# Order of loads and of the modulation pieces at the start of a two-block network turned round

## The reference, cut to what matters

```
s_lat = silu(c);  s_ctx = silu(c_ctx)
sh1, sc1, g1, sh2, sc2, g2 = split(s_lat @ w_mod + b_mod, 6)      # 6 x 1024
csh1, csc1, ...            = split(s_ctx @ w_mod + b_mod, 6)
h  = rms_norm(x,   norm1_g) * (1 + sc1)  + sh1
hc = rms_norm(ctx, norm1_g) * (1 + csc1) + csh1
y  = token_mixers(h, hc, ...)      # h @ w_in, hc @ w_in: attention, a hyena branch, differential attention
x  = x + g1 * y
x  = x + g2 * conv_glu(modulate(rms_norm(x, norm2_g), sh2, sc2), ...)
# hyena filters, from positions alone:
f = sin(freq * (z @ fw1 + fb1)); f = sin(freq * (f @ fw2 + fb2)); f = (f @ fw3 + fb3) * decay, normalised, to spectra
# differential attention: lam = exp(lam_q1 . lam_k1) - exp(lam_q2 . lam_k2) + lam_init
```

## Time and profile before

| | |
|---|---|
| median of 3 runs | 2349.61 us (2344.91 to 2351.23) |
| profiled execution | 2351.88 us, its span 2349.9 us |
| TensorE busy | 2199.5 us, 94% of the span |
| VectorE, ScalarE, GpSimd busy | 1209.5, 429.9, 470.2 us |
| mean granted TensorE clock | 0.960 of full speed |
| first projection matmul | at 58.36 us |

### The profile page before, as it was taken

The page is one execution under the profiler, slowest core; times in us unless marked ns, Lnnn a source line. Parts: engine busy times, 40 slices in busy tenths (PEclk is TensorE's granted clock), DMA queues, the critical chain, the costliest instruction groups (busy, mean ns, idle before and its releaser), DMA issues. The chain is left out here.

```text
span 2349.9 us, 32587 instructions
## 1 busy us (share of the span) xinstructions
PE 2199.5 (94%) x13344; PEld 1962.8 (84%) x13344; DVE 1209.5 (51%) x2470; ACT 429.9 (18%) x1034; POOL 470.2 (20%) x410
## 2 busy tenths in 40 slices
PE   4999779998998999999999998998999999999998
PEld 2466468887667899999999998667899999999998
DVE  2045521112532597887744443542597787844443
ACT  2113320000232112442200000232112443200000
POOL 0000000000000012554433331000012444533331
PEclk7999989999987999999999999997999999999999
DMA  8216213343331378999999995431378999999996
GB/s 334 74 71 249 108 54 142 136 153 135 143 135 54 144 268 338 384 384 392 410 409 409 395 406 222 181 144 54 120 257 338 382 392 386 407 409 409 407 406 252
DMA packets 113525, 616.38 MB, mean 262 GB/s; under 512 B 10201, under 2 KB 10585, under 8 KB 95322
## 3 DMA queue, kind: packets, MB, share of 16 engines
q1 hardware_dynamic: 55578, 403.31, 43.8%
q0 software_dynamic: 57504, 208.82, 23.2%
q10 hardware_dynamic: 288, 2.10, 0.3%
HBM read 612.16 MB, written 2.03 MB: 261 GB/s over the span
## 5 line engine op out<-in xcount | busy, mean ns | idle before, releaser
L390 PE MATMUL psum<-HT,arena 128*128 128x160 f32 (+1 forms) x5984 | 994.3, 327 | 15.5 <-DVE HT L1632 7.1
L390 PEld LDWEIGHTS psum<-HT,arena 128*128 128x128 f32 x5984 | 925.5, 192 | 68.7 <-issue 18.1
L390 PE MATMUL psum<-arena 128*128 128x160 f32 (+6 forms) x5850 | 882.2, 313 | 36.4 <-DMA arena<-in_peer_v 14.4
L390 PEld LDWEIGHTS psum<-arena 128*128 128x128 f32 (+2 forms) x5850 | 817.1, 193 | 85.9 <-issue 32.3
L1950 DVE SCALAR_TENSOR_TENSOR arena<-arena,small 128x1024 f32<-128x1024 f32 x180 | 231.2, 1285 | 293.2 <-DMA arena<-in_peer_v,small 285.9
L2050 POOL DMA_INDIRECT arena<-in_peer_u,small x192 | 245.7, 1279 | 317.7 <-DVE small L1901 280.9
L2050 POOL DMA_INDIRECT arena<-in_peer_v,small x192 | 210.6, 1097 | 357.9 <-PE psum L390 209.3
L1901 DVE CUSTOM_DVE_ANT_0 arena<-arena 128x1024 f32<-128x1024 f32 x192 | 228.1, 1221 | 51.6 <-DMA arena<-in_peer_u,small 45.8
L2056 POOL DMA_DIRECT2D row_tokens<-arena x2 | 1.2, 624 | 1118.9 <-ACT arena L957 1118.9
L390 PE MATMUL psum<-arena,HT 128*128 128x384 f32 (+3 forms) x544 | 202.8, 533 | 17.6 <-ACT HT L1009 10.7
L390 PEld LDWEIGHTS psum<-arena,HT 128*128 128x128 f32 x544 | 108.1, 201 | 105.4 <-issue 48.5
(11 more groups left out here) (226 smaller groups left out, 1003.7 us busy)
## 6 DMA issues: line engine op xcount, KB each, us to landing
arena<-in_peer_ut SPq DMA_DIRECT2D x64, 2048.0 KB
arena<-in_peer_v SPq DMA_DIRECT2D x64, 2048.0 KB
arena<-in_w_mod SPq DMA_DIRECT2D x12, 2048.0 KB
arena<-in_w_in SPq DMA_DIRECT2D x16, 1536.0 KB
arena<-in_w_up SPq DMA_DIRECT2D x11, 2048.0 KB
arena<-in_peer_wq SPq DMA_DIRECT2D x8, 2048.0 KB
arena<-in_w_out SPq DMA_DIRECT2D x6, 2048.0 KB
arena<-in_w_down SPq DMA_DIRECT2D x11, 1024.0 KB
```

What stands on the lines that cost most here:

```text
L390: return pe.matmul(o, a, b, start=start, stop=stop, skip_group_check=True)
```

## The change

The kernel computes the same values. What is different is order, in five places.

1. **Loads.** SP now issues `c`, `cols`, then the first `w_mod` tile, `fw1` and `fw2`, the second tile, `x`, the constants, the third tile, `ctx`, the fourth; `rows`, `fw3`, `decay` and `dft` come behind the first `w_in` tile and `gains` behind the second.
2. **Modulation.** TensorE takes the scales first (tiles 2, 3) and the shifts last (0, 1); `ssx` and `ssc` stand between them.
3. **VectorE** normalises x (`normed_stream(0)`) before the first filter's sine argument and before the shifts, and forms the lambda numbers behind both.
4. **ScalarE** adds the shifts to HT before the second sine, and no longer after it.
5. **Waits.** `h_ready` is now raised for each chunk of HT, and the first projection job waits chunk by chunk; the filter's loads have semaphores of their own (`filters_in` for fw1 and fw2, `windows_in`, `rows_in`).

```diff
@@ TensorE @@
-            pe.wait_ge(s("consts_in"), 16)
-            pe.wait_ge(s("x_squared"), 1)
-            square_sums("ssx", 0)
-            pe.wait_ge(s("ctx_squared"), 1)
-            square_sums("ssc", 1)
             pe.wait_ge(s("silu_c_ready"), 1)
...
+            modulation_rows(2)
+            modulation_rows(3)
+            pe.wait_ge(s("consts_in"), 16)
+            pe.wait_ge(s("x_squared"), 1)
+            square_sums("ssx", 0)
+            filter_1()
+            modulation_columns(2)
+            modulation_columns(3)
             modulation_rows(0)
-            filter_1()
+            pe.wait_ge(s("ctx_squared"), 1)
+            square_sums("ssc", 1)
             modulation_rows(1)
             modulation_columns(0)
-            modulation_rows(2)
             modulation_columns(1)
-            modulation_rows(3)
-            modulation_columns(2)
-            modulation_columns(3)
             filter_2()
-            pe.wait_ge(s("h_ready"), 1)
...
-                    token_job(f"zx{t}{b}", w, HT, b, 0, width)
+                    token_job(f"zx{t}{b}", w, HT, b, 0, width, (s("h_ready"), 0) if (t, b) == (0, 0) else None)
@@ ScalarE @@
+            modulation_row(2)
+            act.wait_ge(s("x_in"), 16)
+            act.activation(SQ[:, 0, :, :], XT[:, :, :], ACT.Square).then_inc(s("x_squared"), 1)
+            modulation_row(3)
+            act.wait_ge(s("consts_in"), 16)
+            root("sq_rooted", rstd[:, 0, :], lambda: jobs.wait_read(act, "ssx"))
+            act.wait_ge(s("ctx_in"), 16)
+            act.activation(SQ[:, 1, :, :], CT[:, :, :], ACT.Square).then_inc(s("ctx_squared"), 1)
             modulation_row(0)
+            root("sq_rooted", rstd[:, 1, :], lambda: jobs.wait_read(act, "ssc"))
+            sine(1, F1)
             modulation_row(1)
-            sine(1, F1)
-            modulation_row(2)
-            modulation_row(3)
-            sine(2, F2)
...
+            jobs.wait_read(act, "mod0")
+            jobs.wait_read(act, "mod1")
             shifted(0, HT, 0)
+            sine(2, F2)
             shifted(1, HC, 0)
+            act.wait_ge(s("lam_dots"), 1)
+            act.activation(lam[:, 2:4], lam[:, 0:2], ACT.Exp).then_inc(s("lam_exps"), 1)
@@ VectorE @@
-            sine_argument(1, "fb1")
-            for t in range(4):
-                modulation(t)
+            dve.wait_ge(s("consts_in"), 16)
+            mean_square("ssx", 0)
+            modulation(2)
+            modulation(3)
             jobs.wait_read(dve, "mod3")
             for n in range(2):
                 gain_and_scale(n, "n1g", 8, n)
             normed_stream(0, HT, XT, 0, 0)
+            mean_square("ssc", 1)
+            sine_argument(1, "fb1")
+            modulation(0)
+            modulation(1)
+            normed_stream(1, HC, CT, 1, 1)
             dve.wait_ge(s("sine_out"), 1)
             sine_argument(2, "fb2")
-            normed_stream(1, HC, CT, 1, 1)
+            jobs.wait_read(dve, "f2")
+            lambda_dots()
             filter_windows()
+            lambdas()
@@ SyncE @@
             for n, tile in enumerate(one):
                 stream(tile, one[n - WSLOTS], tile["src"])
+                if n == 0:
+                    load(FW1[0:33, :], ins["hy_fw1"], "filters_in")
+                    load(FW2[0:64, :], ins["hy_fw2"], "filters_in")
+                if n == 1:
+                    load(XT[:, :, :], ins["x"], "x_in")
+                    load(KON[:, :], ins["consts"], "consts_in")
                 if n == 2:
+                    load(CT[:, :, :], ins["ctx"], "ctx_in")
+                if n == 4:
+                    load(RP[:, :], ins["rows_1"], "rows_in")
...
```

More of the change, by code:

```diff
@@ L447, in filter_3 @@
                 pe.wait_ge(s("sine_out"), 2)
+                pe.wait_ge(s("windows_in"), 48)
                 for b in range(TB):
@@ L505, in _ @@
                 if c0 >= Q_COLS:
-                    pe.wait_ge(s("h_ready"), 2)
+                    pe.wait_ge(s("h_ready"), KC + 1)
                     for b in range(TB):
@@ L657, in up @@
                 w = w.rearrange("p (k n) -> p k n", k=KC)
-                channel_job(f"fa{f}", w, HT, [0, P], range(4), (s("h_ready"), 2) if f == 0 else None)
+                channel_job(f"fa{f}", w, HT, [0, P], range(4), (s("h_ready"), KC + 1) if f == 0 else None)
                 used_up.append(tile)
@@ L963, in free @@
                 return psum_free[jobs.where[name][0]]
[L966 to L970, removed]
-            act.activation(CE[:, :, :], CS[:, :, :], ACT.Exp, scale=-1.0).then_inc(s("silu_exp"), 1)
[L972 to L976, removed]
+            act.wait_ge(s("params_in"), 32)
+            act.activation(CE[:, :, :], CS[:, :, :], ACT.Exp, scale=-1.0).then_inc(s("silu_exp"), 1)
             def modulation_row(t):
                 jobs.wait_full(act, f"modr{t}")
-                if t >= 2:
-                    jobs.wait_full(act, f"mod{t - 2}")
+                if t not in (2, 3):
+                    jobs.wait_full(act, f"mod{t + 2 if t < 2 else t - 2 if t > 5 else t - 4}")
                 act.activation(mod_rows(t), bank(f"modr{t}")[:, :], ACT.Copy).then_inc(free(f"modr{t}"), 1)
@@ L1302, in _ @@
             steps(dve.memset(base[:, :], 0.0))
[L1303 to L1307, removed]
             dve.wait_ge(s("silu_exp"), 1)
@@ L1312, in _, with lambda_dots, lambdas @@
             dve.tensor_tensor(CE4[:, :, 0:2], CE[:, :, :], CS[:, :, :], ALU.mult).then_inc(s("silu_c_ready"), 1)
-            dve.wait_ge(s("lam_exps"), 1)
-            steps(dve.tensor_tensor(lam[:, 4:5], lam[:, 2:3], lam[:, 3:4], ALU.subtract))
-            steps(dve.tensor_scalar(lam[:, 5:6], lam[:, 4:5], LAM_INIT, -1.0, ALU.add, ALU.mult))
-            mean_square("ssx", 0)
-            mean_square("ssc", 1)
+            def lambda_dots():
+                dve.wait_ge(s("rows_in"), 16)
+                steps(dve.tensor_tensor(HTMP[:, 0, 0:HD], RP[:, 0:HD], RP[:, HD:2 * HD], ALU.mult))
+                steps(dve.tensor_tensor(HTMP[:, 1, 0:HD], RP[:, 2 * HD:3 * HD], RP[:, 3 * HD:4 * HD], ALU.mult))
+                dve.tensor_reduce(lam[:, 0:2], HTMP[:, 0:2, 0:HD], AX.X, ALU.add).then_inc(s("lam_dots"), 1)
+            def lambdas():
+                dve.wait_ge(s("lam_exps"), 1)
+                steps(dve.tensor_tensor(lam[:, 4:5], lam[:, 2:3], lam[:, 3:4], ALU.subtract))
+                steps(dve.tensor_scalar(lam[:, 5:6], lam[:, 4:5], LAM_INIT, -1.0, ALU.add, ALU.mult))
             def sine_argument(n, bias):
@@ L1337, in filter_windows @@
             def filter_windows():
-                dve.wait_ge(s("filters_in"), 16 * 5)
+                dve.wait_ge(s("windows_in"), 48)
                 for b in range(TB):
```

21 lines of the change are left out of this document (8 added, 13 removed).

## The result

The changed kernel took 2331.9 us in the median of six runs, the kernel before 2352.8 in six on the same chip; the ratio is 0.9902, 95% interval 0.9876 to 0.9928, so 23 us less (17 to 29). One of the six runs of the changed kernel, of 5868.94 us, counts in no ratio and has no explanation here; the median of the other five is 2330.32. The forecast was 18 us. The profiled execution has a span of 2320.8 us against 2349.9, 29.1 less, at the edge of what the runs allow. Both the 18 and the surplus have to be explained.

A forecast was written before the change was run, and what follows sets the result against it. TensorE is busy 94% of the span, so the first projection's start sets the time. Loads 7.3 us plus chain 11.0 gave 18.4, rounded to 18 off the median 2349.61: 2331.6 us, range 2325.6 to 2340.6.

The forecast's parts named there:

- The start carries everything behind it: First projection on TensorE, at 58.36 us: bringing it forward moves more than 2290 us of later work as one piece.
- Loads in order, 7.3 us: Load queue delivers in order of issue; last w_mod tile lands at 32.2 instead of 39.52 us, 7.3 us earlier.
- rival 2: Load queue shares its rate among all issued transfers, first tile lands near 27 us; gain 10, 2339.5 us; chance 0.06.
- The chain, 11.0 us: From last w_mod tile's landing to first projection, over the engines: 7.8 us instead of 18.8, gaining 11.0.
- The copy behind the sine, a new wait: ScalarE's copy of tile 1's rows queues behind the first sine: ready at 36.1, made from 37.5 to 38.1 us.
- `filter_3` not waited for: TensorE's filter_3 needs the second sine, ready at 47.2 us; the zx0 jobs ahead end at 49.7 at the earliest.
- The clock: TensorE's start jobs: gain 24.0 us at full clock, 9.8 at half; first projection pair kept at 13.64 us.
- The mixed sum: TensorE's start jobs partly at full, partly at half clock, tile 0's rows at 2.8 us; gain 18.4 us.
- Rival 1: TensorE at half clock through most of the start; gain 8 to 14 us, near 2339; chance 0.13.
- rivals 3 and 4: Behind the start: 3, an unseen wait hands gain back, chance 0.12; 4, half clock in projections, up to 2370 us, 0.04.
- The size: Whole kernel: 18.4 us gained at the first projection, rounded down to 18, for a median of 2331.6 us.

The follow-up runs named there:

- loads-alone kernel: Kernel before with rows, fw3, decay, dft loaded behind the first w_in tile, gains behind the second, lambda numbers later; other order old; ratio 0.9962.
- after: First profile of the changed kernel, no further edit: first projection at 39.74 us, span 2320.8 us; timed ratio 0.9902.
- with the sums first: Changed kernel with small loads ahead of the weight tiles and ssx, ssc first on TensorE; not timed in rounds, projection gain 13.6 us against kernel before.
- order-alone run: Changed kernel with all small loads back ahead of the weight tiles (gains behind the third), new order of work kept; ratio 0.9964.
- after2: Second profile of the changed kernel, no edit: first projection at 38.77 us, span 2328.2 us; timed ratio 0.9907.
- after3: Third profile of the changed kernel, no edit: first projection at 38.82 us; timed ratio 0.9918.
- before: First profile of the kernel before the change: first projection at 58.36 us, span 2349.9 us; timed median 2352.8 us.
- the last experiment: Changed kernel with fourth tile's copy before first sine, filter_2 behind first projection job, x and constants behind first w_mod tile, ctx behind second, sums earlier; ratio 0.9944.

## Why the prediction came true, step by step

- **The start carries everything behind it.** Right. 18.6 us at the projection, gapless stretches behind it.
- **Loads in order, 7.3 us.** Right. A tile has landed at the last increment of its load semaphore in the trace: the four `w_mod` tiles at 9.79 (8.7 forecast, the one landing that was off by over 1 us), 14.76 (14.4), 24.63 (24.9) and 32.02 (32.2); the constants released ssx at 19.78 (19.8). The fourth tile came 7.45 us earlier than before (39.47). The forecast needed no more than that the landings come in the order of issue, and all of these and the 6.9 us of the loads-alone kernel fit that; rival 2, with the first tile near 27, falls.
- **The chain, 11.0 us.** Right as a sum for the changed kernel: from the fourth tile's landing to the projection 7.7 us against 7.8 forecast, and 18.9 before. Two misses cancel in it: the rows started 1.1 us sooner than forecast (33.07, not 34.2), and from there it took 6.7 us and not 5.8, with columns and `filter_2` at half rate in `after`. Nor is all of the gain order: the fourth tile's rows and the last columns took 3.64 and 3.58 us before and 1.92 and 2.87 now, so some 2.4 us are the clock. Read as something that the order gives by itself it would be wrong: alone it gave 6.5 us, with the sums first 13.6. The working did not say so, and the expectation of the order-alone run, which added the terms, missed by 3.9 us.
- **The copy behind the sine, a new wait.** Right, and 0.97 us long.
- **`filter_3` not waited for.** Right, with 5.5 us to spare.
- **The clock.** The mixed sum was the right case. Tile 0's rows took 1.92 and not 2.8; the last columns and `filter_2` ran at half rate in `after` and at full in `after2` and `after3`, a swing of 1 us. The zx0 pair, costed at an unchanged 13.64, took 12.62, 12.25 and 10.56, and 12.45 and 12.15 in the two later profiles of the kernel before: so the 13.64 was the odd one. On the means of three, 12.75 and 11.81, the pair gave 0.9 us more. Rival 1 did not come about. The Trainium skill's rule behind it (TensorE: Matmul & The Clock Gate, HAM oscillation), by which each burst behind a wait for transfers begins at half rate, was borne out in part: the second tile's rows, after waits of 1.2 to 1.5 us, took 1.92 in `after` and `after3` and 3.64 in `after2`. The waits that the page tells of are longer than these.
- **Handed back, or slower (rivals 3 and 4).** Neither. No later wait took the gain, and the clock was back at 44.
- **The size.** 18 forecast, 19 to 23 timed on three occasions; the start's 18.9 and the pair's 0.9 make 19.8. That the forecast of 2331.6 and the measured 2331.9 agree so closely is luck: the forecast was counted from the 2349.61 of three runs, and beside the changed kernel the one before took 2352.8. With the first ratio 2349.61 would have become 2326.6, and its 23 us are the upper end of the 14 to 23 that the forecast allowed itself. The profiled 29.1 is not evidence for more: 9 to 10 us of it are the clock's chance behind the start.

Granted clock and TensorE's busy time from the changed kernel's trace (us, PE busy, clock, DMA share, GB/s), which answer to the earlier trace rows:

```profile
20.40:23.80 3.40, 3.40 (x11) 0.56 0.96 407
23.80:37.40 13.60, 12.62 (x84) 0.99 1.01 393
37.50:44.20 6.70, 6.70 (x16) 0.52 1.02 410
44.30:60.00 15.70, 15.70 (x47) 1.00 0.77 311
```

From 23.8 to 37.4 TensorE is busy 93% and at full clock; the half clock of 27 us that `before` had around the projection's start has shrunk to 6.7; each trace has 3.4 us of it earlier as well.

## What to carry to other kernels

Where one queue feeds the start of a program, what is not needed for the first dense stretch belongs behind what is, and the engines' orders must be turned so that nothing whose data is there stands behind what still travels. The loads alone and the order alone gave 7.8 and 6.5 us here, 4 less than both at once, because ready sums stood behind late tiles; with the sums first the order alone gave 13.6. Late small loads together with the sums first were not run in this form. Look for the short instruction that waits in front of a long stream on an in-order engine; a sine of 0.42 us here, waiting for its argument, held up the shifts by 7.4 us. And before a surplus in one profile is explained, profile the same kernel again: by matching equal instructions of two traces one sees at once whether a difference arises where the change was made.

## What had not been expected

- The same binary differs by up to 16 us of 2290 behind the same point, with 132.4 to 174.1 us at half rate. Two profiles can't resolve less than about 10 us by their spans here, though they agree within 1 us (the changed kernel) to 2 us (the one before) on when the first projection starts.
- The clock view shows 1.00 for the first stretches, while durations say half rate: in the last experiment ssx ran 6.62 us from 16.27 to 22.89 (3.72 at full rate) under this row of us, PE busy, clock, DMA share and GB/s:

```profile
16.20:22.90 6.70, 6.63 (x17) 1.00 1.02 428
```

The granted clock's record has its first entry only at 22.2 us in this trace, and between 12.8 and 22.8 us in the six profiles of the two kernels; ahead of it the view shows 1.00. There the durations are the safer reading. So the 0.79 and 0.91 of the first slices say nothing of the clock in their first 13 us.
